# Query norm folded into the scaling of the scores, rotary factor as a quotient, and two moves in the written order of the first attention

## The reference, cut to what matters

```
q = (rms_norm(c_q, q_a_norm) @ w_uq).reshape(B, S, 8, 128 + 64)
q_nope = rms_norm(q[..., :128], q_nope_norm)
q_pe = rope(rms_norm(q[..., 128:], q_rope_norm), cos, sin)
logits = (q_nope . k_nope + q_pe . k_pe) / sqrt(192)        # causal mask
out = softmax(logits) @ v
```

## Time and profile before

| | |
|---|---|
| median of three runs | 895.45 us |
| span of the profiled execution | 893.8 us |
| TensorE busy | 882.5 us (99%) |
| weight loads busy | 767.7 us (86%) |
| VectorE, ScalarE, GpSimd busy | 633.2, 523.2, 41.0 us |
| TensorE on the chain that ended last | 94% |

### The profile page before, as it was taken

How to read it: one execution, slowest core, us unless ns; L and a number is a source line. 1 busy time by engine, 2 the same in 40 slices (tenths; PEclk the granted TensorE clock), 3 DMA queues, 4 the chain that set the end, 5 groups by cost and what they waited for, 6 DMA issues and landing times.

```text
span 893.8 us, 13052 instructions
## 1 busy us (share of the span) xinstructions
PE 882.5 (99%) x5231; PEld 767.7 (86%) x5231; DVE 633.2 (71%) x1047; ACT 523.2 (59%) x855; POOL 41.0 (5%) x72
## 2 busy tenths in 40 slices
PE   9999999999999999999999999999999999999997
PEld 8888888888888888888888888999989998798885
DVE  6897876766575666567656556679899867767774
ACT  6998444453454577645444445466556756747782
POOL 0151000000000000000000000000014310000000
PEclk9999999999999999999999999999999999999999
DMA  8732545554644454447555655455251312654511
GB/s 305 232 111 62 209 161 209 184 176 160 247 171 166 165 176 150 144 133 249 185 188 170 217 193 174 146 187 161 78 187 48 111 55 56 228 212 142 188 48 47
DMA packets 60877, 143.73 MB, mean 161 GB/s; under 512 B 4497, under 2 KB 6673, under 8 KB 60817
## 3 DMA queue, kind: packets, MB, share of 16 engines
q1 hardware_dynamic: 60816, 142.91, 47.0%
HBM read 141.85 MB, written 1.05 MB: 160 GB/s over the span
## 4 chain that ended last, share of the span: by engine, by line
PE 94%; ACT 3%; DVE 2%; DMA 1%; issue 1%; SPq 0%; DVEq 0%
PE ps L509 89%; PE ps L517 5%; ACT arena L1440 1%; DMA raw<-mla_w_in_dram 1%; ACT xhl L1440 0%; ACT whi L1440 0%; DVE arena_r L2426 0%; DVE sub L2426 0%; DVE arena L2426 0%; DVE wlo L2426 0%; DVE X L2432 0%; DVE st L2432 0%; ACT L1443 0%; ACT st L1440 0%; SPq L3810 0%
## 5 line engine op out<-in xcount | busy, mean ns | idle before, releaser
L2426 DVE TENSOR_TENSOR wlo<-raw,whi 128x2048 fp32r<-128x2048 f32 (+4 forms) x141 | 300.2, 2137 | 109.0 <-ACT whi L1440 108.8
L1440 ACT ACTIVATE whi<-raw 128x2048 fp32r<-128x2048 f32 (+6 forms) x143 | 251.8, 1771 | 165.1 <-PE ps L509 150.3
L509 PE MATMUL ps<-xhl,whi 128*128 128x512 f32 (+1 forms) x912 | 214.0, 348 | 0.0
L509 PE MATMUL ps<-whi,xhl 128*128 128x512 f32 (+2 forms) x528 | 167.2, 385 | 1.8 <-DVE xhl L2432 1.3
L509 PE MATMUL ps<-whi,oth 128*128 128x512 f32 x416 | 165.2, 397 | 0.0
L509 PEld LDWEIGHTS ps<-xhl,whi 128*128 128x128 f32 x912 | 149.8, 188 | 14.8 <-DVE xhl L2432 0.2
L509 PE MATMUL ps<-whi,otl 128*128 128x512 f32 x416 | 162.4, 390 | 0.0
L509 PE MATMUL ps<-wlo,oth 128*128 128x512 f32 x416 | 162.2, 390 | 0.0
L509 PE MATMUL ps<-xhl,wlo 128*128 128x256 f32 x704 | 135.6, 281 | 0.0
L509 PEld LDWEIGHTS ps<-xhl,wlo 128*128 128x128 f32 x704 | 115.2, 189 | 10.8
L509 PEld LDWEIGHTS ps<-whi,xhl 128*128 128x128 f32 x528 | 98.5, 189 | 20.1 <-issue 2.8
(11 more groups left out here) (146 smaller groups left out, 830.8 us busy)
## 6 DMA issues: line engine op xcount, KB each, us to landing
raw<-mlp_w_in_dram SPq DMA_DIRECT2D x32, 1024.0 KB, 5.3
raw<-mlp_w_out_dram SPq DMA_DIRECT2D x32, 1024.0 KB, 4.9
raw<-gdn_w_in_dram SPq DMA_DIRECT2D x16, 1024.0 KB, 5.3
raw<-moba_w_qkv_dram SPq DMA_DIRECT2D x12, 1024.0 KB, 5.3
raw<-kv_w_dram SPq DMA_DIRECT2D x8, 1024.0 KB, 5.5
raw<-fox_w_in_dram SPq DMA_DIRECT2D x8, 1024.0 KB, 5.1
raw<-mla_w_o_dram SPq DMA_DIRECT2D x4, 1024.0 KB, 5.8
raw<-moba_w_o_dram SPq DMA_DIRECT2D x4, 1024.0 KB, 6.1
```

Source lines behind the costliest of these rows:

```text
L509: return eng.matmul(o, l, r, start=start, stop=True, skip_group_check=True)
L1440: return eng.activation(o, i, f, **kw)
L2426: return eng.tensor_tensor(o, a, b, f)
```

## The change

VectorE's `q_norm` goes. `q_scales` takes its place: w / sqrt(192), and w'/w by a reciprocal and a product, on four columns each. It signals `s_hn` as `q_norm` did. For rounds 0 and 2 it stands earlier in VectorE's list (before `k_sums(0)`, and before `o_lo` 0 and 1). `q_T` now waits for the copied queries (`s_uq`) and no longer for the norm; `q_rope` waits for `q_scales` and multiplies by the quotient. `logits` scales with w / sqrt(192), which differs between the two tiles of tokens, so its one instruction of 384 columns becomes two, of 128 and 256. In the lists of round 1, TensorE's `q_T(1)` goes ahead of `turn_p(0)`; ScalarE's `divide(0)` goes ahead of `exp(1)` and `q_copy(1)` ahead of `rsq("mla_k1")`, `qp_copy(1)` and `p_copy(1)`. No DMA is moved.

```diff
--- before.py
+++ after.py
@@ -375,6 +375,7 @@
         for n_ in ("k0", "k1", "q0", "q1", "q2", "q3"):
             SM["ss", "mla_" + n_] = tile_(8)
             RT["mla_" + n_] = rsq_tiles(8)
+        q_scale, q_ratio = [tile_(4) for _ in range(4)], [tile_(4) for _ in range(4)]
         for h in range(8):
             SM["mla", h] = [tile_(2) for _ in range(4)]
         pre_ss = {"mla": ss0}
@@ -850,7 +851,7 @@
                 heads_T("mla", f"k{g}", j, lambda t, i: kvtok[:, t, 4 * g + 2 * j + i, 0:128], s_hn, HN["mla", f"k{g}"])
 
             def q_T(i):
-                heads_T("mla", f"q{i}", 0, lambda t, i_: qtoks[i % 2][:, 2 * t + i_, 0:128], s_hn, HN["mla", f"q{i}"])
+                heads_T("mla", f"q{i}", 0, lambda t, i_: qtoks[i % 2][:, 2 * t + i_, 0:128], s_uq, 2 * i + 2)
 
             def qp_T(i):
                 L.wait_ge(s_qp, i + 1)
@@ -1075,9 +1076,9 @@
             to(9, 0)
             score_pair(0)
             to(10, 0)
+            q_T(1)
             turn_p("mla", 0)
             qp_T(1)
-            q_T(1)
             turn_p("mla", 1)
             value("mla", 0)
             value("mla", 1)
@@ -1898,14 +1899,14 @@
             q_squares(2)
             exp("mla", 0)
             k_copy(0, 1)
+            divide("mla", 0)
             exp("mla", 1)
-            divide("mla", 0)
             divide("mla", 1)
             p_copy("mla", 0)
+            q_copy(1)
             rsq("mla_k1")
             qp_copy(1)
             p_copy("mla", 1)
-            q_copy(1)
             uq_copy(3, 0)
             rsq("mla_q2")
             o_hi("mla", 0)
@@ -2518,7 +2519,10 @@
                     L.wait_ge(s_ex, J - 1)
                 if stage == "mla":
                     L.wait_ge(s_pr, 16)
-                    stt(S, b[:, 0:384], float(1.0 / np.sqrt(192.0)), K("mask"), ALU.mult, ALU.add).then_inc(s_sx, 1)
+                    L.wait_ge(s_hn, HN["mla", f"q{j // 2}"])
+                    f = [q_scale[j // 2][:, 2 * t + j % 2:2 * t + j % 2 + 1] for t in range(2)]
+                    stt(S[:, 0:128], b[:, 0:128], f[0], K("mask")[:, 0:128], ALU.mult, ALU.add)
+                    stt(S[:, 128:384], b[:, 128:384], f[1], K("mask")[:, 128:384], ALU.mult, ALU.add).then_inc(s_sx, 1)
                 else:
                     bias = biasM[:, j, :] if stage == "moba" else bb[j % 4]
                     L.wait_ge(s_rq, (0 if stage == "moba" else 2) + j // 4 + 1)
@@ -2748,12 +2752,15 @@
                 ts(m[:, 0:4], ss[:, 0:4], 1.0 / 128, EPS, ALU.mult, ALU.add)
                 ts(m[:, 4:8], ss[:, 4:8], 1.0 / 64, EPS, ALU.mult, ALU.add).then_inc(s_rm, 1)
 
-            def q_norm(i):
+            def q_scales(i):
+
                 n_ = f"mla_q{i}"
                 rsq_done(n_)
-                qn = qtoks[i % 2][:, :, 0:128]
-                tt(qn, qn, bc(RT[n_][5][:, 0:4].unsqueeze(2), 2, 128), ALU.mult).then_inc(s_hn, 1)
-
+                w = RT[n_][5]
+                ts(q_scale[i], w[:, 0:4], float(1.0 / np.sqrt(192.0)), None, ALU.mult)
+                L.step(eng.reciprocal(q_ratio[i], w[:, 0:4]))
+                L.settle()
+                tt(q_ratio[i], w[:, 4:8], q_ratio[i], ALU.mult).then_inc(s_hn, 1)
 
             def variance(i):
                 L.wait_ge(s_ssq, 2 + 2 * i)
@@ -3162,15 +3169,15 @@
             q_sums(0)
             lo(8)
             rsq_b("mla_q0")
+            q_scales(0)
             k_sums(0)
-            q_norm(0)
             rsq_b("mla_k0")
             k_norm(0)
             q_sums(1)
             lo(9)
             kp_copy()
             rsq_b("mla_q1")
-            q_norm(1)
+            q_scales(1)
             k_sums(1)
             logits("mla", 0)
             logits("mla", 1)
@@ -3181,15 +3188,15 @@
             rsq_b("mla_k1")
             k_norm(1)
             rsq_b("mla_q2")
+            q_scales(2)
             o_lo("mla", 0)
             o_lo("mla", 1)
-            q_norm(2)
             logits("mla", 2)
             logits("mla", 3)
             q_sums(3)
             picks()
             rsq_b("mla_q3")
-            q_norm(3)
+            q_scales(3)
             over_sum("mla", 2)
             over_sum("mla", 3)
             logits("mla", 4)
@@ -3727,9 +3734,9 @@
             def q_rope(i):
                 n_ = f"mla_q{i}"
                 L.wait_ge(s_cos, 2)
-                L.wait_ge(s_rs, RSQ[n_] + 1)
+                L.wait_ge(s_hn, HN["mla", f"q{i}"])
                 qp = qtoks[i % 2][:, :, 128:192]
-                L.step(tt(qp, qp, bc(RT[n_][5][:, 4:8].unsqueeze(2), 2, 64), ALU.mult))
+                L.step(tt(qp, qp, bc(q_ratio[i].unsqueeze(2), 2, 64), ALU.mult))
                 L.settle()
                 q4 = qtoks[i % 2].rearrange("p (t h) n -> p t h n", t=2)
                 if i >= 2:
```

## The result

| | before | after |
|---|---|---|
| median of 20 runs each | 895.41 us | 897.72 us |
| lowest and highest | 894.31, 897.13 | 896.46, 900.13 |
| span of the profiled execution | 893.8 us | 895.2 us |

The ratio is 1.0023, with an interval of 1.0016 to 1.0030: slower by 2.1 us (1.4 to 2.7). 897.15 had been forecast, as "same" with 0.56 and "slower" (above 897.24) with 0.41; the median lies above that line.

A forecast was written before the change was run, and what follows sets the result against it. TensorE's list was taken as the bound, with ScalarE's full chain deciding its wait in the first attention. Terms 1.0 + 0.37 + 0.34 = 1.7 us put the median at 897.15 us, from 895.45; range 894.9 to 898.5.

The forecast's parts named there:

- Term 1: First attention, heads 0 and 1: value 1 on TensorE starts 1.0 us later (bounds 0.2 to 1.3), and the delay stays.
- The maxima: Part of the delay at value 1: the split scaling on VectorE makes the maxima 0.18 us later.
- The hole: Part of the delay at value 1: ScalarE idles behind exp 1 until the reciprocal is made, costing 0.30 us.
- The query copy in front: Part of the delay at value 1: ScalarE copies queries 1 ahead of the copy of probabilities 1, costing 0.52 us.
- Term 2: Heads 4 and 5: later maxima delay exp 5 and the copies scores 6 wait for, +0.37 us (0 to 0.68).
- Term 3: Heads 6 and 7: later maxima delay output 4's low part, which frees value 6's bank, +0.34 us (0 to 0.65).
- The 0.18 for the split: VectorE's scaling of the scores, as two instructions, takes 0.74 us instead of 0.56, by the last attention's pair.
- a new wait of its own: Rival, 0.18: narrow margins at round 3's rotary work, query turn 2's bank and probabilities 3 break; +1.1 us more, 898.25.
- The gain stays: Rival, 0.08: TensorE keeps what the early query turn and division give at value 1, up to 1.3 us; 894.1.
- A wash: Rival, 0.14: the delay at value 1 is only 0.2 and the two later ones total 0.4; +0.6 us, 896.05.
- The busy share misleads: Rival given no chance: TensorE's matmul busy share is a poor measure; weight loads at 86% would leave room for gains.
- GpSimd, taken as nothing: GpSimd's rotary work ends -0.1 to +0.45 us later; counted as nothing, with 0.3 kept for the range.

The follow-up runs named there:

- the scaling alone: The change with round 1's lists on TensorE and ScalarE in their former order, scaling still in two: 896.56 us, ratio 1.0012.
- taking the move back: The change with ScalarE's division 0 put back behind exp 1, one run: 897.74 us.
- The order alone: The kernel before with only the new order of TensorE's and ScalarE's lists, query norm and one scaling as before: 896.59 us, ratio 1.0011.
- the scaling in one instruction: The change with one scaling pass over 384 columns, using the first tile's factor for both tiles: 896.53 us, ratio 1.0012.
- the copy put back: The change with ScalarE's query copy 1 put back behind the copy of probabilities 1, one run: 899.88 us.

## Why the prediction was right, and where it was not

**What bounds it: right.** Waits of TensorE for ScalarE decide the stretch. Filling TensorE's own wait moved nothing in its list; the moves in ScalarE's list did. One sentence of it was too strong: that everywhere else from 33 to 95 us one matmul follows on the other. TensorE also stands for 0.35 us at 35.27, for VectorE's part of a weight chunk; it does so in both kernels (0.36 in the change), so nothing hangs on it.

**Term 1, 1.0 us: measured 0.94.** Its parts came out too. The maxima: the scaling alone gives 0.18 at value 1. The hole: 0.23 us seen, and 0.28 by taking the move back, against 0.30. The query copy in front: 0.48 from its start (56.89 in the trace, the second of the two in the row from 56.52) to the next start at 57.37, against 0.52. The order alone gives 0.78 where the parts have 0.82. Of the forecast times, with the 0.22 taken off: division 1 at 55.83 (55.81), the turn of probabilities 1 at 56.68 (56.66), value 1 at 58.56 to 58.63 (58.52), the key turn at 61.6 (61.54). The copy of probabilities 1 starts 5.5 us after exp 0; 5.6 had been said.

**Term 2, 0.37: measured 0.37** at scores 6 itself (1.03 just before, 1.40 there). Ahead of it the list had lost another 0.09, 0.06 of it at the first transpose of query turn 2, in the change and in the scaling alone, and not in the order alone or with the scaling in one instruction. That is the bank freed by the longer scaling, whose margin of 0.04 the working had put among the new waits and priced at 0.2. **Term 3: 0.34 measured, 0.34 said.** In both the scaling in one instruction took away most.

**The 0.18 for the split** was right as a sum and wrong as to its parts. The pair in the last attention gives the right number for another reason in part: both shapes there already read their operand from memory, and the row of 384 columns that it was held against the earlier trace rows has a constant. The scaling in one instruction separates 0.06 for the factor read and 0.12 to 0.13 for the split. The 0.125 us for a further instruction from PSUM, an estimate from the 120 cycles at 0.96 GHz that the Trainium skill gives (VectorE: DVE Perf Modes, section The TRN2 errata), is what was measured for the split alone; on that the trace agrees, and my doubt of it was due to the factor.

**What the working did not have: the granted clock.** The forecast took TensorE's time between waits as fixed. The change's three waits within 4 us were followed in one of its two profiles by 3.4 us at half clock, worth 1.4 us. By their mean clocks 13 of 27 executions had a fall somewhere, and their median is 1.3 us above that of the others. That this moved the median from about 896.9 to 897.72 fits the counts but is argued. The time forecast, 897.15, lies between the two groups, 0.57 below the median and within its range; of this distance none is in the three terms, and it is no larger than the noise. Of the classes the likelier, "same", did not come; with a forecast 0.09 below the line that was close to a toss-up. The rival "a new wait of its own" has a time near that of the group with low clocks (898.25 against 898.2) by coincidence, and the wrong mechanism: GpSimd did not hold a matmul up, and query turn 2 waited 0.06 us for its bank, not 0.2.

**The rivals.** *The gain stays* turned on the chain from exp 0 to the copy of probabilities 1 being under 4.76 us; it is 5.5. *A wash* wanted term 1 at 0.2. *The busy share misleads* would have left room for gains elsewhere; at 99% busy every delay of the list came through to the end (1.74 us at value 6, 1.66 at the end).

**GpSimd, taken as nothing: right.** It starts later, and runs faster. In round 3 it is done at 71.63 and the rotary transposes start at 71.73: of the margin of 0.17 before, 0.10 is left. It was close: the weight load of these transposes does wait for GpSimd, 0.22 us in the change and 0.16 before, and only the matmuls behind it have no gap.

```profile
PEld ps L518 <- POOL arena L3732: 0.2, 1, 0.2
```

GpSimd's first rotary instruction, mean of the four:

```profile
L3732 POOL TENSOR_TENSOR arena<-arena,st 128x256 f32<-128x256 f32 x4 | 2.5, 616 | 52.4 <-DVE st L2427 52.4
```

All four now take 0.62. Before, two took 0.62 and two, the ones beside the long multiplication, 1.12, and the mean was 870 ns. The page's 39.1 us busy against 41.0 agrees.

## What to carry to other kernels

Where an engine without a hole in its list is the bound, moving its calls shifts the wait; only work taken off it, or off the chain that feeds it, shortens one. An instruction that used to stand between a sum and the division by it was cover for the round trip over another engine: look at what fills such a gap before it is moved away. And a wait of TensorE of a microsecond or two can be followed by a lower clock, which one profile may not show: take the clock of all the runs, and when it varies, profile again, since the mean doesn't say where it fell.

## What the runs showed of the hardware

- TensorE's granted clock fell from 2.4 to 1.2 GHz for 3.4 us behind a stretch in which it was busy 2.34 of 3.90 us (no single wait above 1.4 us), which cost 1.4 us; behind the same waits it stayed at 2.4 in four other profiles (2.35 of 3.90 us busy). It fell again behind 3.25 of 5.80 us busy with the copy put back. By the runs' mean clocks 13 of 27 executions of the change had a fall somewhere, and 0 of 11 with the wait filled by matmuls without a reader. What decides which execution falls stays open; no run was made for it.
- A scalar read from memory in place of a constant costs a 384-column instruction of VectorE from PSUM 0.06 us (614 against 555 ns).
- A two-input instruction of GpSimd over 256 elements took 1.12 us where it started beside a two-input one of VectorE with both inputs in SBUF (0.69 us long, at 48.8 and 65.8 us), and 0.62 us beside a reduction (40.8) and beside VectorE's subtractions with one input in PSUM (59.7).
